# The feed-forward's second product by seven block products instead of eight

## The reference

```
def _sq_relu_mlp(h, w1, w2):
    return jnp.square(jax.nn.relu(h @ w1)) @ w2

h_lat = h_lat + g2 * _sq_relu_mlp(_modulate(_rms_norm(h_lat, norm2_g[i]), sh2, sc2), mlp_w1[i], mlp_w2[i])
if not last:   # the context tokens, in layer 0 only
    h_ctx = h_ctx + cg2 * _sq_relu_mlp(_modulate(_rms_norm(h_ctx, norm2_g[i]), csh2, csc2), mlp_w1[i], mlp_w2[i])
```

## Time and profile before

| | |
|---|---|
| runs, median (lowest to highest) | 2651.51 us (2648.1 to 2653.54) |
| profiled execution, its own time | 2646.01 us |
| its span, first to last instruction | 2644.3 us |
| mean granted TensorE clock | 0.972 |
| TensorE busy | 2446.0 us, 93%, 12100 matmuls |
| VectorE busy | 1389.7 us, 53% |
| ScalarE busy | 852.5 us, 32% |
| GpSimd busy | 537.4 us, 20% |
| first and last matmul of the two `mlp` stages (attention lies between) | 387.0 and 2634.0 us |

### The profile page before, as it was taken

One profiled execution on the slowest core, in us unless ns is written; L12 is line 12 of the kernel. 1 busy time (PEld: TensorE's weight loads), 2 busy tenths in 40 slices (PEclk: granted clock), 3 DMA queues, 4 the chain that ended last, 5 costly groups with the idle time before them and its releaser, 6 DMA issues. The chain is left out here.

```text
span 2644.3 us, 33894 instructions
## 1 busy us (share of the span) xinstructions
PE 2446.0 (93%) x12100; PEld 2001.2 (76%) x12100; DVE 1389.7 (53%) x2325; ACT 852.5 (32%) x1472; POOL 537.4 (20%) x335
## 2 busy tenths in 40 slices
PE   4998989999999999999769688887989999999999
PEld 2667857888888888888567576665668888888887
DVE  4546766344443444434677688883273444344344
ACT  4452134121111211112343488882152121212121
POOL 0000031112111121111200256661122222222220
PEclk9998998999999999999989899999989999999999
DMA  6437520101101001010121211102011111111101
GB/s 233 151 112 269 210 94 32 48 32 34 45 32 48 32 33 46 32 48 0 64 95 44 68 29 28 28 9 111 32 64 48 48 48 48 48 53 47 59 32 64
DMA packets 74683, 171.51 MB, mean 65 GB/s; under 512 B 36992, under 2 KB 47744, under 8 KB 64128
## 3 DMA queue, kind: packets, MB, share of 16 engines
q1 hardware_dynamic: 67952, 137.73, 15.1%
q0 software_dynamic: 3456, 25.17, 2.6%
q10 hardware_dynamic: 3216, 7.86, 0.9%
HBM read 158.16 MB, written 12.58 MB: 65 GB/s over the span
## 5 line engine op out<-in xcount | busy, mean ns | idle before, releaser
L916 DVE SCALAR_TENSOR_TENSOR ht<-l_yy_ps,mod,ht 128x512 f32<-128x512 f32 (+1 forms) x640 | 445.5, 697 | 310.0 <-PE l_yy_ps L53 309.5
L51 PE MATMUL l_z_ps<-nh,l_w1h 128*128 128x512 f32 (+1 forms) x1280 | 478.1, 374 | 12.1 <-DVE nl L58 11.3
L52 PE MATMUL l_z_ps<-nl,l_w1h 128*128 128x512 f32 (+1 forms) x1280 | 474.5, 371 | 0.0
L53 PE MATMUL l_z_ps<-nh,l_w1l 128*128 128x512 f32 (+1 forms) x1280 | 474.1, 370 | 0.0
L51 PE MATMUL l_yy_ps<-l_ah,l_w2h 128*128 128x512 f32 (+1 forms) x1280 | 471.3, 368 | 2.1 <-DVE l_al L58 2.1
L52 PE MATMUL l_yy_ps<-l_al,l_w2h 128*128 128x512 f32 (+1 forms) x1280 | 471.1, 368 | 0.0
L53 PE MATMUL l_yy_ps<-l_ah,l_w2l 128*128 128x512 f32 (+1 forms) x1280 | 470.9, 368 | 0.0
L897 DVE TENSOR_TENSOR l_sq<-l_rel 128x512 f32<-128x512 f32 x160 | 118.9, 743 | 569.5 <-ACT l_rel L808 569.4
L51 PEld LDWEIGHTS l_z_ps<-nh,l_w1h 128*128 128x128 f32 x1280 | 244.1, 191 | 59.9 <-DVE nl L58 16.1
L53 PEld LDWEIGHTS l_z_ps<-nh,l_w1l 128*128 128x128 f32 x1280 | 244.2, 191 | 40.5
L52 PEld LDWEIGHTS l_z_ps<-nl,l_w1h 128*128 128x128 f32 x1280 | 244.3, 191 | 40.3 <-issue 0.5
(11 more groups left out here) (204 smaller groups left out, 3491.6 us busy)
## 6 DMA issues: line engine op xcount, KB each, us to landing
l_w1f<-w SPq DMA_DIRECT2D x32, 1024.0 KB, 4.7
l_w2f<-w SPq DMA_DIRECT2D x32, 1024.0 KB, 4.9
maw<-ada SPq DMA_DIRECT2D x24, 1024.0 KB, 5.2
aw<-ada POOLq DMA_DIRECT2D x24, 1024.0 KB, 5.0
qb<-queries SPq DMA_DIRECT2D x64, 128.0 KB, 2.7
fw<-fnet_w SPq DMA_DIRECT2D x8, 512.0 KB, 5.1
fx<-x SPq DMA_DIRECT2D x8, 512.0 KB, 5.1
park<-ht SPq DMA_DIRECT2D x1, 4096.0 KB, 12.0
```

What stands on the lines that cost most here:

```text
L51: pe.matmul(out, lh, rh, start=first, stop=False)
L52: pe.matmul(out, lh, rl, start=False, stop=False)
L53: return pe.matmul(out, ll, rh, start=False, stop=last)
L916: dve.scalar_tensor_tensor(out=h, in0=y_ps[u % 4][:, 0:n], scalar=mod[:, layer, G2, m, v:v + 1], in1=h, op0=ALU.mult, op1=ALU.add).then_in ...
```

## The change

Only latent tokens and only the second product are changed in what is computed; the order of nearly everything in `mlp` moves with it. Write the pair's part of `w2` as a 2 x 2 of blocks A: rows for the output halves (512 features each), columns for the two hidden halves c (128 each). Write the squared relu as B: rows for c, columns for the two token blocks of 512. The product A B (2 x 2 blocks) is done with seven block products in place of eight:

The core of the diff, first the weights and ScalarE's and GpSimd's queues:

```diff
-                def high1(p):
-                    act.wait_ge(s_w1, p * 16 + 16)
-                    act.wait_ge(s_z, p * U1 + PRE)
-                    act.activation(w1h[:], w1f[:], ACT.Copy).then_inc(s_w1h, 1)
+                def high1(p, c):
+                    act.wait_ge(s_w1, p * 32 + 16 * (c + 1))
+                    act.activation(w1h[:, c], w1f[:], ACT.Copy).then_inc(s_w1h, 1)
...
+                def high2(p, name):
+                    if name in SUM_AT:
+                        act.wait_ge(s_sum, p * 4 + (PRE + SUM_AT[name]))
+                    else:
+                        act.wait_ge(s_w2, p * 32 + 32)
+                    act.activation(w2h[:, RING[name]], w2f[:, PLACE[name]], ACT.Copy).then_inc(s_w2h, 1)
...
+                def outputs(p, order, more):
+                    if more:
+                        act.wait_ge(s_z, p * U1 + (PRE + U1))
+                        high1(p + 1, 1)
+                    high(p, "B21", order)
+                    high2(p, "S2")
+                    high(p, "T4", order)
+                    high2(p, "S3")
+                    act.wait_ge(s_y, p * NG + (PRE + Y_AT[("ctx", 1) if C else ("M1", 3)] + 1))
+                    for name in W_ORDER[6:]:
+                        high2(p, name)
+
+                def pair(p, more=True):
+                    relu(p, "B11", Z_LOOP)
+                    high(p, "B11", Z_LOOP)
+                    for name in ("S1", "A11"):
+                        high2(p, name)
+                    relu(p, "B12", Z_LOOP)
+                    high(p, "T1", Z_LOOP)
+                    for name in ("A12", "S4"):
+                        high2(p, name)
+                    if C:
+                        relu(p, "C0", Z_LOOP)
+                        high(p, "C0", Z_LOOP)
+                    if more:
+                        high1(p + 1, 0)
+                    relu(p, "B22", Z_LOOP)
+                    for name in ("B22", "T2", "T3"):
+                        high(p, name, Z_LOOP)
+                    relu(p, "B21", Z_LOOP)
...
+                def weights(p):
+                    pool.wait_ge(s_w2, p * 32 + 32)
+                    summed(p, "S1", "A21", ALU.add, "A22")
+                    low2(p, "S1")
+                    pool.wait_ge(s_w2l, p * NW + (PRE + 1))
+                    summed(p, "S2", "S1", ALU.subtract, "A11")
+                    low2(p, "A11")
+                    pool.wait_ge(s_w2l, p * NW + (PRE + 2))
+                    summed(p, "S3", "A11", ALU.subtract, "A21")
+                    low2(p, "A12")
+                    pool.wait_ge(s_w2l, p * NW + (PRE + 3))
+                    summed(p, "S4", "A12", ALU.subtract, "S2")
+                    low2(p, "S4")
...
+                with pool.Fori(1, PAIRS - 1) as p:
+                    weights(p)
+                    low1(p + 1, 0)
+                    outputs(p, True)
```

VectorE's queue and TensorE's groups:

```diff
+                def acc(p, prod, m):
+                    c, h = chunk(prod, m)
+                    dve.wait_ge(s_y, y_at(p, prod, m))
+                    if EARLIER[prod]:
+                        dve.wait_ge(s_acc, p * NA + (PRE + ACC_TO[EARLIER[prod], m]))
+                    dve.scalar_tensor_tensor(out=h, in0=y_ps[m][:], scalar=mod[:, layer, G2, c, 0:1], in1=h,
+                                             op0=ALU.mult, op1=ALU.add).then_inc(s_acc, 1)
...
+                def hidden(p):
+                    square(p, "B11", Z_LOOP)
+                    low(p, "B11", HI_LOOP)
+                    square(p, "B12", Z_LOOP)
+                    diff(p, "T1", "B12", "B11", Z_LOOP, HI_LOOP)
+                    low(p, "T1", HI_LOOP)
+                    if C:
+                        square(p, "C0", Z_LOOP)
+                        low(p, "C0", HI_LOOP)
+                    square(p, "B22", Z_LOOP)
+                    diff(p, "T2", "B22", "T1", Z_LOOP, HI_LOOP)
+                    diff(p, "T3", "B22", "B12", Z_LOOP, HI_LOOP)
+                    for name in ("B22", "T2", "T3"):
+                        low(p, name, HI_LOOP)
+                    square(p, "B21", Z_LOOP)
...
+                def outputs(p, zorder, horder, final=False):
+                    dve.wait_ge(s_acc, p * NA + PRE)
+                    for m in range(4):
+                        acc(p, "M5", m)
+                    diff(p, "T4", "B21", "T2", zorder, horder)
+                    acc(p, "M3", 0)
+                    low(p, "B21", horder)
+                    for m in range(1, 4):
+                        acc(p, "M3", m)
+                    acc(p, "M2", 0)
+                    low(p, "T4", horder)
+                    for g in GROUPS[Y_AT["M2", 1]:]:
...
+                def group(p, g, horder):
+                    prod, m = g
+                    freed(p, g)
...
+                    pe.matmul(y_ps[m][:], wh, a_h, start=first, stop=False, skip_group_check=not first)
+                    pe.matmul(y_ps[m][:], wh, a_l, start=False, stop=False, skip_group_check=not first)
+                    pe.matmul(y_ps[m][:], wl, a_h, start=False, stop=True, skip_group_check=not first).then_inc(s_y, 1)
```

More of the change, by code:

```diff
@@ L713, in mlp @@
     N = f"l{layer}_"
-    U1, U2 = 2 * NB, KC * NB
-    NZ = 3 if NB == 3 else 4
+    C = NB == 3
+    NZ = 3 if C else 4
     RMS_AT = 5
     SQ = 4
-    with ExitStack() as ph:
[L719 to L725, removed]
+    TOK = {"B11": (0, 0), "B12": (1, 0), "B21": (0, 1), "B22": (1, 1), "C0": (2, 0), "C1": (2, 1)}
@@ new lines, in _ @@
+                act.wait_ge(s_nl, 2 * KC)
+                relu(0, "B11", Z_FIRST)
+                high(0, "B11", Z_FIRST)
+                for name in ("A12", "S4"):
+                    high2(0, name)
+                if C:
+                    norm(2)
+                relu(0, "B21", Z_FIRST)
+                relu(0, "B12", Z_FIRST)
+                high(0, "T1", Z_FIRST)
+                relu(0, "B22", Z_FIRST)
+                for name in ("B22", "T2", "T3"):
+                    high(0, name, Z_FIRST)
@@ L864, in _ @@
+                outputs(last, Z_LOOP, False)
+                if out is not None:
+                    for i in range(len(HALVES)):
+                        if not ON_DVE[i]:
+                            out_half(i)
             @block.vector
@@ L902, in out_tile @@
[L902 to L919 removed]
+                    low_n(b * KC + KC - 1)
@@ L1000, in _, with hidden @@
[L1000 to L1007 removed]
+                def hidden(p, order, first=False):
+                    for pos, name in enumerate(order):
+                        b, c = TOK[name]
+                        t0, n = TB[b]
+                        if pos == 0 or first and c == 1 or order[pos - 1][0:1] != "C" and TOK[order[pos - 1]][1] != c or name == "B22":
+                            pe.wait_ge(s_w1l, p * 2 + (PRE + c + 1))
+                        pe.wait_ge(s_rel, p * U1 + (PRE + pos - NZ + 1))
+                        for k in range(KC):
+                            if first:
+                                pe.wait_ge(s_nl, b * KC + k + 1)
+                            last = mm3(pe, z_ps[pos % NZ][:, 0:n], (w1h[:, c, k], w1l[:, c, k]),
+                                       (nh[:, k, t0:t0 + n], nl[:, k, t0:t0 + n]), k == 0, k == KC - 1)
+                        last.then_inc(s_z, 1)
```

455 lines of the change are left out of this document (286 added, 169 removed).

## The result

The changed kernel is slower: median 2731.34 us (2728.09 to 2734.13, four runs) against 2652.48 us beside it, a ratio of 1.0300, 95% interval 1.0282 to 1.0318. The forecast was 2690, in a range of 2646 to 2730. The sign was right and the size was not: +79 us where +39 was forecast.

The account below looks back on a forecast made before the run. TensorE's issue rate was taken as the bound before, with VectorE's late first eviction deciding after the change: 2646.0 + 36 - 1 + 4 = 2685, plus 5.5 for the median, 2690.5; own range 2660 to 2725, overall 2646 to 2730.

Parts of the forecast that it names:

- Ends: **+4: First and last pairs of both layers and the tail: +4 us together, bounds -2 and +9.
- layer 1's +36: Layer 1's 14 steady pairs: a late first eviction makes each 46.1 us against 43.52, +2.6 us, +36 in all.
- layer 0's steady pairs: 14 steady pairs of layer 0: -0.6 us each by the chain, 0.5 back for the clock, -1 us in all.
- the 5.5 us that were added for the median: Whole kernel: median of runs 5.5 us above the profiled execution, so 2685 became 2690.5.
- Layer 0's start: First pair of layer 0, put together with the tail at +1 us.
- Layer 1's first pair: First pair of layer 1: ScalarE stands behind the S4 chain before the other relus, about +4.5 us.
- The steady chain of layer 1: Steady pair of layer 1, step by step: S4's sum, relu and square of B22, first eviction at 26.55 us, end at 46.1.
- the third rival: Slower still: VectorE's pitch is 0.75 us, 2730, or TensorE's clock falls in most pairs, 2746; chance 0.11.
- The signs: What would show the forecast in the trace: layer 1 pairs of 45 to 47 us, TensorE idle 2 to 4 us before M3.
- The first rival: Short chain, faster: first eviction at 23.2 us, layer 1 pair 42.2, if square B22 ends before about 19.5; 2617, chance 0.12.
- its 0.667: VectorE's output evictions: one taken to cost 0.667 us from start to start, though each lasts 0.75.

Follow-up runs that it names:

- e1: Changed kernel with GpSimd's low part of layer 0's second first-product weight half issued behind the last context square: 2723.13 us, ratio 1.0285 to the kernel before.
- c4: Changed kernel with the orders of e1, e2 and e3 together: 2664.23 us, ratio 1.0070 to the kernel before.
- c6: Changed kernel with e1, e2 and ScalarE's S1 and A11 copies ahead of relu B11 in layer 1's steady pairs: 2654.28 us, ratio 1.0036.
- c7: Changed kernel with all orders of e1, e2, e3, c6, plus first-pair copies inside the second norm and layer 0's first-pair weight half behind B21: 2650.67 us.
- e3: Changed kernel with ScalarE's S4 copy moved behind the high part of B22 in layer 1: 2727.26 us, ratio 1.0308 to the kernel before.
- e2: Changed kernel with layer 1's next first weight half moved into the output phase and the second to its end: 2681.45 us, ratio 1.0129.
- e5: Changed kernel with twelve unused matmuls per layer 1 pair but the last: 2758.01 us behind the wait for M3's bank, 2714.64 us ahead of it.
- e8: Changed kernel with seven eighths of GpSimd's first-weight-half low part left out in layer 1's steady pairs, ScalarE's copy kept: 2697.63 us, ratio 1.0178.
- c8: The kernel of c7 with the orders in layer 0's steady pairs too, except A11's: 2638.93 us, ratio 0.9962 to the kernel before.

## Why the prediction was wrong

The step that failed is the term "Ends: **+4**". It measured +29.2 (15.2 - 2.3 + 16.1 + 0.2). The second is layer 1's +36, which measured +52.4. On the profiled execution, 2685 forecast and 2732.3 measured, they are 25 and 16 of the 47; layer 0's steady pairs add 2 and the untouched stretch 3.6. (On the medians, 2690.5 and 2731.3, the miss is 41: the 5.5 us that were added for the median were not there after.)

- **Layer 0's start** was put at "+1". The prediction walked a steady pair instruction by instruction and the first pairs not at all. The row was there before: ten squares in a block of 11.09 us. The new low part stands in the middle of that queue and waits for a copy behind the norm. e1 shows the wait (19.5 us; the same order in c4 and c6 gives 17.3 and 20.9) and also that only 4 to 5 us of it count by itself, because the next thing in ScalarE's queue, S4's copy and the context block's norm ahead of the second relu, then holds the pair for 11.6 us. The other part, 6.88 us of waiting for B21 behind a weight load, was in no step either; c7 took it away.
- **Layer 1's first pair** was put at +4.5 for the S4 chain alone; its hidden phase measured 42.6 us against 34.2 before, its output phase 29.7 against 21.9. With S4 moved (e3) the hidden phase is 38.9, so that term is about 3.7. A part that was in no step is again the second weight half ahead of B21's high part: with the halves late (e2) the output phase is 22.9. But the two do not add: c4 has both orders, and its pair (65.0) is no shorter than e2's (65.3), since its output phase takes 26.1 us, with TensorE waiting 2.1 us inside it and a mean granted clock of 0.83 (0.90 in e2's). Every changed kernel keeps some 9 us or more over the 56.1 before; why stays open.
- **The steady chain of layer 1** was right in its mechanism and nearly in its numbers, each step 0.5 to 0.7 us late: end of GpSimd's S4 18.0 forecast and 18.6 measured, end of relu B22 20.15 against 20.7, end of its square 22.85 against 23.53, first eviction 26.55 against 27.19. GpSimd's 512-column piece, of which six stand in that chain, was taken at 1.2 and measured 1.29 to 1.30 undisturbed, above the stated bound of 1.28. With the clock whole (e5 ahead of the wait) the pair is 46.59 against 46.1: 0.5 us, 7 in 14 pairs.
- **The clock** was set aside in the third rival with "evictions wait for VectorE then, not for matmuls". At half clock matmuls started 0.43 us apart, 1.3 us for a group of three where an eviction takes 0.66, and it cost 0.67 us a pair, 9.4 in all. A hole of 3 us was forecast in so many words, and the price of it left out.
- **Layer 0's steady pairs** (-1 forecast, +1.0 measured) came near by luck. The forecast was 0.6 us under 55.08 by the chain and 0.5 back for the clock. The clock took nothing, it is 1.00 in the window of this stretch, and the chain came out at 55.15, 0.07 over: two errors of about 0.6 us cancel.
- **The signs**: the eviction pace of 0.66 (four in 2.72 us), TensorE idle between M5 and M3 (3.52 us), squares of up to 2.9 us and layer 0 pairs of 54 to 56 came as forecast; a pair of layer 1 at 47.26 lies just above "45 to 47".
- **The first rival**, a shorter chain and a faster kernel, is no rival of this kernel but a description of the next one. It said 42.2 us a pair from a square of B22 done before about 19.5; c6 has it done at 19.6 and the pair at 42.67.

The Trainium skill, "SBUF — State Buffer", section "Who interferes with whom", says that a VectorE instruction with two SBUF inputs contends with a GpSimd one that reads SBUF, that the shared port is an exclusive lock, and that the order of issue decides who blocks. The rows agree: the square listed at 2363.80 ends 0.55 us after GpSimd's end at 2366.06, so one tensor read twice acts as two inputs here, and e8 takes most of the delay away by shortening GpSimd alone. The evictions from PSUM keep 0.74 us on the mean (0.75 before).

The prediction sets a rule of the Trainium skill against its 0.667, "VectorE: DVE Perf Modes", section "The DRAIN you can't avoid". The same section also says that a next operation that is not held starts earlier, which the prediction leaves out; the evictions 0.66 us apart, listed at 0.74, agree with that sentence.

## What to carry to other kernels

When a change lengthens a chain across three in-order queues, ask of each queue what stands ahead of the critical instruction and whose wait it inherits; then do the same for the first iteration, whose order is another. Saved work on the engine that bound the kernel before is worth nothing where it only widens a hole (idle time between two waits): put the work back into the hole to see, and count the clock behind it. Work for an engine that shares a port goes beside operations that don't use the port (here, beside the evictions from PSUM), and moving either side of a collision without the other may only move the collision.

## What was not expected

Twelve unused matmuls in each of 15 pairs made the kernel faster, by 14 us by the ratios and 10.7 between the profiled executions. The identity's own worth here, orders mended, is 0.9 us a pair in layer 1 and 0.7 in layer 0 (c8: 42.61 and 54.35 against 43.52 and 55.08) where TensorE saves 2.7. No run was made for the rest, but the trace of c8 shows where most of it lies: TensorE still waits ahead of M2 for VectorE's low part of B21, in every steady pair, here one of layer 0 and one of layer 1.

```profile
711.36 0.50 PE L1252 MATMUL l_yy_ps<-l_ah,l_w2h 128*128 128x512 f32 x1 [1.37 <-DVE l_al L58]
...
2139.65 0.50 PE L1252 MATMUL l_yy_ps<-l_ah,l_w2h 128*128 128x512 f32 x1 [0.94 <-DVE l_al L58]
```

In c8 the first pairs still take 75.8 and 69.9 us against 71.9 and 56.1 before.
